# Five small moves in a fused two-block transformer kernel: accumulator banks for one pair of weight chunks, a later broadcast of 1/rms, later loads of gain rows, two head scalings in a row

## The reference

```python
def rmsnorm(x, g, eps=NORM_EPS):
    y = x32 * lax.rsqrt(jnp.mean(x32 * x32, axis=-1, keepdims=True) + eps)
    return (y * g.astype(jnp.float32)).astype(x.dtype)

def swiglu(h, w_up, w_down):
    gate, up = jnp.split(h @ w_up, 2, axis=-1)
    return (jax.nn.silu(gate) * up) @ w_down

# first_block, layer 0: the very first work of the program
x = x + 0.5 * swiglu(rmsnorm(x, norm_g[i, 0]), ffn_w_up[i, 0], ffn_w_down[i, 0])
...
return rmsnorm(x, final_norm_g)          # end of the first block

# second_block
h = rms_norm(x, g_pre_mix[l])            # a norm of a norm
proj = h @ w_in[l]
mq, mk, mv, rq, rk, rv, rg = jnp.split(proj, SPLIT_POINTS, axis=-1)
...
ro = retention(rq, rk, split_heads(rv, RET_HEADS))
ro = ro * lax.rsqrt(jnp.mean(ro * ro, axis=-1, keepdims=True) + NORM_EPS)
ro = jax.nn.silu(rg) * merge_heads(ro).astype(x.dtype)
mix = jnp.concatenate([mo, ro], axis=-1) @ w_out[l]
x = x + rms_norm(mix, g_post_mix[l])
...
x = x + rms_norm(c, g_post_cross[l])
h = rms_norm(x, g_pre_ffn[l])
```

## Time and profile before

| what | value |
|---|---|
| median of 3 runs | 1496.78 us |
| profiled execution | 1497.63 us |
| its span (first to last instruction) | 1495.8 us |
| PE busy | 1458.8 us (98%), 7412 matmuls |
| DVE, ACT, POOL busy | 829.6, 689.0, 45.0 us |
| chain that ended last | PE 95%; ACT, DVE, DMA, SPq 1% each |
| DMA | 262.14 MB, mean 175 GB/s |

### The profile page before, as it was taken

The page is one execution under the profiler, slowest core; times in us unless marked ns, Lnnn a source line. Parts: engine busy times, 40 slices in busy tenths (PEclk is TensorE's granted clock), DMA queues, the critical chain, the costliest instruction groups (busy, mean ns, idle before and its releaser), DMA issues.

```text
span 1495.8 us, 18732 instructions
## 1 busy us (share of the span) xinstructions
PE 1458.8 (98%) x7412; PEld 1228.4 (82%) x7412; DVE 829.6 (55%) x927; ACT 689.0 (46%) x899; POOL 45.0 (3%) x96
## 2 busy tenths in 40 slices
PE   7999999999999999999999999999899999899997
PEld 5888889988888888888888788888787889688886
DVE  4554566855545555445666465545765555454554
ACT  5455354454443544435445454344443444444342
POOL 1000000000000000000000000000101100000000
PEclk9999999999999999999999999999999999899999
DMA  9555554445555455554543356554433544255551
GB/s 353 221 197 181 188 177 169 160 169 197 197 186 184 165 200 195 191 181 163 172 152 128 113 197 235 187 197 169 155 113 117 179 168 142 99 197 181 187 195 57
DMA packets 38574, 262.14 MB, mean 175 GB/s; under 512 B 4288, under 2 KB 4544, under 8 KB 7648
## 3 DMA queue, kind: packets, MB, share of 16 engines
q1 hardware_dynamic: 37152, 252.85, 48.0%
q0 software_dynamic: 1344, 8.16, 1.4%
HBM read 259.95 MB, written 1.05 MB: 174 GB/s over the span
## 4 chain that ended last, share of the span: by engine, by line
PE 95%; ACT 1%; DVE 1%; DMA 1%; SPq 1%; issue 1%; POOL 0%; DVEq 0%; POOLq 0%; ACTq 0%
PE prod L994 15%; PE prod L996 15%; PE prod L995 15%; PE acc L994 9%; PE acc L996 9%; PE acc L995 9%; PE prod L988 4%; PE prod L989 4%; PE prod L990 4%; PE acc L1160 2%; PE aux L1024 2%; DMA raw<-in_weights_dram 1%; PE acc L1011 1%; PE acc L1179 1%; ACT acts_h L1311 1%
## 5 line engine op out<-in xcount | busy, mean ns | idle before, releaser
L1481 DVE TENSOR_TENSOR w_lo<-raw,w_hi 128x2048 fp32r<-128x2048 f32 x235 | 538.4, 2292 | 334.6 <-ACT w_hi L1293 334.3
L1293 ACT CAST w_hi<-raw 128x2048 fp32r<-128x2048 f32 x235 | 449.1, 1912 | 294.8 <-PE acc L996 184.3
L994 PE MATMUL prod<-w_hi,acts_h 128*128 128x512 f32 x960 | 383.6, 400 | 10.5 <-DVE four L1596 7.0
L996 PE MATMUL prod<-w_hi,acts_l 128*128 128x512 f32 x960 | 376.0, 392 | 0.0
L995 PE MATMUL prod<-w_lo,acts_h 128*128 128x512 f32 x960 | 375.7, 391 | 0.0
L994 PE MATMUL acc<-w_hi,mix_h 128*128 128x512 f32 x600 | 237.5, 396 | 2.7 <-DVE sq L1766 2.4
L996 PE MATMUL acc<-w_hi,mix_l 128*128 128x512 f32 x600 | 234.2, 390 | 0.0
L995 PE MATMUL acc<-w_lo,mix_h 128*128 128x512 f32 x600 | 234.2, 390 | 0.0
L994 PEld LDWEIGHTS prod<-w_hi,acts_h 128*128 128x128 f32 x960 | 181.4, 189 | 52.6 <-issue 9.6
L996 PEld LDWEIGHTS prod<-w_hi,acts_l 128*128 128x128 f32 x960 | 181.1, 189 | 38.6
L995 PEld LDWEIGHTS prod<-w_lo,acts_h 128*128 128x128 f32 x960 | 181.6, 189 | 35.8 <-issue 0.5
(11 more groups left out here) (248 smaller groups left out, 1194.5 us busy)
## 6 DMA issues: line engine op xcount, KB each, us to landing
raw<-in_weights_dram SPq DMA_DIRECT2D x235, 1024.0 KB, 4.9
raw<-in_weights_dram SPq DMA_DIRECT2D x12, 256.0 KB, 7.0
work<-in_mem_dram POOLq DMA_DIRECT2D x2, 1024.0 KB, 13.3
grow<-in_gain_rows_dram POOLq DMA_DIRECT2D x4, 512.0 KB, 3.8
tabs<-in_tabs_dram POOLq DMA_DIRECT2D x1, 1696.0 KB, 8.8
work<-in_x_t_dram SPq DMA_DIRECT2D x4, 256.0 KB, 5.9
x_res<-in_x_dram SPq DMA_DIRECT2D x1, 1024.0 KB, 8.7
work<-in_mem_t_dram POOLq DMA_DIRECT2D x1, 1024.0 KB, 14.3
```

The source lines that it names most:

```text
L994: pe.matmul(out, still_hi, wh, start=first, stop=False, skip_group_check=True)
L996: return pe.matmul(out, still_lo, wh, start=False, stop=last, skip_group_check=True)
L1293: act.copy(w_hi[:, c % RING], raw[:, c % RAW]).then_inc(hi_done, 1)
L1481: dve.tensor_tensor(w_lo[:, c % RING], raw[:, c % RAW], w_hi[:, c % RING].bitcast(F32), ALU.subtract).then_inc(lo_done, 1)
```

## The change

Five edits. First, chunks 2 and 3 write `acc[2]` and `acc[3]` in place of the product banks (`up_bank`), chunk 2 no longer waits for a free bank, and the down chunk 4 waits for `mid_done` 4 before it writes `acc[2]`; with this, x is loaded behind the quarters of chunk 2 and squared behind their rounding. Second, at the double norm the spread stands amid the "k" chunk. Third, POOL issues the load of the next gain row behind the next statistic in place of ahead of it (three of four loads; the one at the first statistic stays). Fourth, `late` issues all scales that are due (`while` for `if`). Fifth, `scale_x` stands ahead of the `rg` chunks.

```diff
-        if self.scales < self.sums and not self.hold:
+        while self.scales < self.sums and not self.hold:
             self.pl.head_scale(...)
             self.scales += 1
...
     pl.project(w, 0, "q", 0)
-    pl.spread("x")
-    pl.project(w, 512, "k", 0)
+    pl.project(w, 512, "k", 0, mid=lambda: pl.spread("x"))
...
     pl.ready_v(ret)
+    pl.add("scale_x", stat=pl.stat)
     pl.project_tokens(w, 2560, "rg", 0, mid=slot, between=lambda: end(slot))
     norms.hold = False
     end(slot)
-    pl.add("scale_x", stat=pl.stat)
...
+        def up_bank(it, t):
+            return acc[2 + t] if it["c"] in (2, 3) else prod_flat[(it["e"] + t) % 2]
...
             # SyncE
-            sp.dma_start(x[:], A["x"]).then_inc(x_loaded, 16)
             for k in range(4):
                 sp.dma_start(raw[:, 2, quarter(k)], weights[2][:, quarter(k)])...
+            sp.dma_start(x[:], A["x"]).then_inc(x_loaded, 16)
...
             # GpSimd
                 if kind == "stat":
                     statistic(it)
+                    if next_row:
+                        done, count, row = next_row
+                        pool.wait_ge(done, count)
+                        pool.dma_start(grow[:], A["gain_rows"][row]).then_inc(gain_row_loaded, 16)
+                        next_row = None
...
                 elif kind == "second_squares":
-                    pool.wait_ge(xf_done, 4)
-                    pool.dma_start(grow[:], A["gain_rows"][1]).then_inc(gain_row_loaded, 16)
+                    next_row = (xf_done, 4, 1)
                 elif kind == "post_sums" and it["row"] < 3:
-                    pool.wait_ge(y_copied, it["y_copied"] + 4)
-                    pool.dma_start(grow[:], A["gain_rows"][it["row"] + 1]).then_inc(gain_row_loaded, 16)
+                    next_row = (y_copied, it["y_copied"] + 4, it["row"] + 1)
...
             # TensorE
-                    if k_half == 0:
+                    if k_half == 0 and it["c"] != 2:
                         reader(pe, it["free"][t])
-                        mm = token_passes(prod_flat[e % 2], ...)
+                        mm = token_passes(up_bank(it, t), ...)
...
+                    if b == 2 and it["c"] == 4:
+                        pe.wait_ge(mid_done, 4)
...
             # ScalarE, first_prep (Silu and DVE's product read up_bank too)
+                    for k in range(4):
+                        split_piece(2, k)
+                    state["split"] = RAW
                     act.wait_ge(x_loaded, 16)
                     for b in range(4):
                         ins = square(x[:, t, cols], b, 0)
-                    for k in range(4):
-                        split_piece(2, k)
-                    state["split"] = RAW
```

More of the change, by code:

```diff
@@ L1049, in tokens_chunk @@
                 for t in parts:
-                    e = it["e"] + t
-                    if k_half == 0:
+                    if k_half == 0 and it["c"] != 2:
                         reader(pe, it["free"][t])
@@ L1058, in tokens_chunk @@
                             piece_ready(it["c"], k)
-                        mm = token_passes(prod_flat[e % 2], slot, k * 512, hi[:, base + kt, tokens(t)],
+                        mm = token_passes(up_bank(it, t), slot, k * 512, hi[:, base + kt, tokens(t)],
                                           lo[:, base + kt, tokens(t)], kt == 0, kt == KT - 1)
@@ L1345, in _ @@
                                 act.wait_ge(mid_done, 2 * m + t - 1)
-                            act.activation(gate_s[:, t], prod_flat[(it["e"] + t) % 2][:, 0:S], ACT.Silu,
+                            act.activation(gate_s[:, t], up_bank(it, t)[:, 0:S], ACT.Silu,
                                            scale=rstd["x"][:, t:t + 1]).then_inc(silu_done, 1)
@@ L1596, in _ @@
                             dve.scalar_tensor_tensor(
-                                out=mid_tok[m % 2][:, t], in0=prod_flat[(it["e"] + t) % 2][:, S:2 * S],
+                                out=mid_tok[m % 2][:, t], in0=up_bank(it, t)[:, S:2 * S],
                                 scalar=rstd["x"][:, t:t + 1], in1=gate_s[:, t], op0=ALU.mult, op1=ALU.mult
```

## The result

The changed kernel takes 1478.75 us (median of 4 runs, 1478.37 to 1480.98); the kernel before, timed again beside it, 1497.48 (4 runs, 1493.32 to 1499.19). The ratio is 0.9875, 95% interval 0.9863 to 0.9887: faster by 1.1 to 1.4%. The forecast was 1481.7, so the direction and the range (1476 to 1489) held. The sum said 15.1 us gained; 18.7 were, from 1497.48. The profiled execution took 1478.86 us, its span is 1477.0. One execution of the kernel before in a later session, 2442.22 us at a granted clock of 0.556, belongs to a slow state and is left out of every comparison.

A forecast was written before the change was run, and what follows sets the result against it. PE, busy 98% of the span, bounds the kernel, its waits costing twice through the clock. 5.1 + 4.4 + 1.6 + 4.0 = 15.1 us off 1497.63 gives 1482.5, the median 0.85 lower: 1481.7; range 1476 to 1489.

The forecast's parts named there:

- Banks: First FFN: with other banks for chunk 2, pair 0's transpose starts 7.1 us earlier; 5.1 taken, ends 0 and 7.1.
- If the gap of 2.0 us lowers the clock, as that of 1.8 did, 2.0 us are lost again: First FFN, PE's new gap ahead of pair 0's transpose: a lower clock loses 2.0 us, leaving 5.1.
- 1/rms at 24.4: First FFN: squares end at 22.5, POOL's last operation 1.9 us behind; 1/rms at 24.4, before ACT is free at 24.60.
- Spread: Double norm: spread amid "k" cuts PE's wait from 4.60 to 1.7 us; 4.4 gained if the clock holds, else 2.9.
- Gain rows: Norm behind the cross attention: POOL starts 1.6 us earlier, PE waits 4.0 for 5.6; 1.6 gained, 0 elsewhere.
- Heads: End of retention: both scales early, so PE's 2.4 us wait and 1.6 of low clock go; 4.0 gained.
- The port: Double norm: DVE and POOL share an SBUF port pair exclusively, so moving the load gains 0; without the rule about 1.2.
- Supply: Rival, first FFN: x, squares and 1/rms late, or later weight chunks no sooner; 4 us lost, 1485.7; chance 0.14.
- Load in place of port: Rival, double norm: the load slowed the statistic, not DVE's remainder; spread 1.2 us earlier, 1480.5; chance 0.08.
- No wait over 1 us appeared between 1060 and 1180: Sign for the second block: such a wait would make the forecast wrong; new-wait rival 1490.1, chance 0.07.
- the clock never stayed low: Rival, first FFN: PE stays at 1.2 GHz behind the new 2.0 us gap, slower than before, 1512.7; chance 0.03.

The follow-up runs named there:

- e4: The changed kernel with one scale a slot again (`if` for `while`), scale_x still early; 1482.28 us.
- e2: The changed kernel with the spread ahead of "k" again at the double norm; 1484.29 us.
- e7: The changed kernel with DVE's remainder beside POOL's first operation at the double norm cut into four instructions of 512 columns; 1478.79 us.
- e10: The changed kernel with scale_x behind the scales of heads 0 and 1 again; 1478.73 us.
- e12: The changed kernel with the edits of e8 and e9 together; 1475.49 us.
- e8: The changed kernel with 14 unread 128x512 matmuls in PE's 4.0 us wait at the norm behind the cross attention; 1475.92 us.
- e3: The changed kernel with the gain rows loaded ahead of the statistics again; 1480.88 us.
- e9: The changed kernel with DVE's whole remainder at the double norm put behind POOL's statistic; 1476.73 us.
- e5: The changed kernel with banks kept, but x loaded and squared ahead of chunk 2's quarters as before; 1480.35 us.
- e1: The changed kernel with its first edit undone whole: chunks 2 and 3 in product banks, x loaded and squared ahead of chunk 2; 1486.36 us.
- e6: The changed kernel with the new load order kept, but chunks 2 and 3 in the product banks; 1485.11 us.

## Why the prediction was right, and where its size was off

Undone singly the parts cost 7.6, 5.5, 2.1 and 3.5 us in the medians, together 18.7, and the whole change brought 18.7. That these agree so well is partly luck. In the stages and waits that the edits touch, the four cost 6.7, 4.2, 1.6 and 2.4, together 14.9; the rest is clock in places that the edits leave alone, and e4 leaves `scale_x` early, so it isn't the whole of the two edits at retention. What bears the argument is each place by itself:

1. **Banks** (forecast 5.1, measured 7.6 at the double norm, 1036.47 for 1044.07, and 6.7 when undone alone). The mechanism was right to the wait: chunk 2 without a wait, a gap of 2.0 (2.15) at `turn_mid`, chunk 5 in time. The term that was mis-sized is "If the gap of 2.0 us lowers the clock, as that of 1.8 did, 2.0 us are lost again". It didn't in this profile, and that it didn't is chance. Of nine executions with that gap in their profile (after, e2 to e4, e7 to e10, e12) it fell in three, e2, e8 and e12, and its price there was 1.5 to 1.6, not 2.0. The other half microsecond is the product, which ends at 27.06 in place of the forecast 27.71, since chunk 3 could be rounded 0.66 earlier. That is scatter of the first loads too: over these nine kernels the transpose starts between 26.81 and 28.10, always 7.7 to 7.8 behind chunk 2, which starts between 19.07 and 20.39. The forecast had 1/rms at 24.4, with POOL's last operation as slow as before; it came at 23.4, and nothing waited for it.
2. **Spread** (4.4, measured 4.4: 12.01 less the 7.60 from the banks). The clock held behind 1.69 us, here and in all eight other kernels with a gap of 1.7 to 1.9 there: all have 3.41 to 3.43 from spread to rope.
3. **Gain rows** (1.6, measured 1.74 up to the transposes; 0 at the double norm, measured 0). Another 0.76 came in the stage behind the transposes, 6.82 for 7.58, which the forecast had left at zero. It swings with the clock there (6.82 to 7.92 in kernels that still wait), so it isn't shown to belong to the change.
4. **Heads** (4.0, measured 4.25). The while loop alone does it all (e10), and `scale_x` does nothing beside it. Undone alone the loop costs 2.39 in its stage (e4), not 4.25: the wait of 2.12 is back, but the clock held behind it. Of the 1.86 between e4 and before, 0.28 is the shorter wait and nearly all the rest the clock, which may hold or fall behind such a gap. The reason I gave for the wait of before, `scale_x` and a remainder between the scales, was half right: the remainder makes nearly all of it.
5. **The port.** The rule of the Trainium skill (SBUF — State Buffer, "SBUF: two separate sides") by which I took 0 at the double norm holds: e3 shows the 0, e9 the other side of it, 1.18 us for moving DVE's instruction out of the way. The e7 trace shows that the rule says too little about parts back to back.
6. **Rivals.** Supply: chunk 5 landed in time with the new order, and late without it (e5), so the danger was real and the second half of the first edit removed it. Load in place of port: refuted by the changed kernel itself, where POOL's first operation took 1.38 with no load ahead of it, and by e9. No wait over 1 us appeared between 1060 and 1180, and the clock never stayed low.

In sum 15.1 was forecast and 18.8 measured in the profiles: 2.5 from the banks, 0.8 behind the cross attention's transposes, 0.3 from retention, 0.1 from the rows. So the forecast's direction, places and waits were right by its mechanism; that its sum was 3.6 short is, for 2.0, the toss of the clock in one place.

## What to carry to other kernels

Cut the trace at events that every version has and compare stage by stage: parts of 1 us then show singly in one profile, where medians of runs scatter by 2. Look at the clock of each stage before you put a difference down to an edit. When a wait goes, work out the next one on the same engine and the loads that it will lean on; a bank that is free earlier is worth little if the slot behind it is freed late. A long wait of TensorE that can't be removed can be filled with unread matmuls (1.8 to 2.9 us at a wait of 4.0; nothing measurable at waits of about 2). A long VectorE operation with two inputs in SBUF belongs behind, not beside, a small GpSimd chain that TensorE waits for (1.2 us here).

## What the runs showed of the hardware that I had not expected

- The same gap doesn't always bring the same clock. At mem_v PE waited 1.80 to 1.83 us in 13 kernels; the clock fell behind it in six profiled executions (before, after, e2, e7, e10, e12) and held in seven (e1, e3 to e6, e8, e9). In e12 the window behind it:

```profile
1203.00:1206.00 3.00, 3.00 (x9) 2.29 (x9) 2.45 (x2) 0.00 (x0) 0.00 (x0) 0.53 1.00 396
```

  Behind the 2.1 in the first FFN it was three of nine, behind the 1.7 to 1.9 at the spread none of nine. It held behind 2.12 (e4, retention) and 2.24 (e5, chunk 4) and fell behind 2.40 (before); behind 3.6 to 5.6 it was low each time, in e4 only from about 2 us after the gap. A fall behind a gap near 2 us costs about 1.6 us. For such gaps a forecast should take a share of it, not all or nothing.
- The scatter of the kernel before goes with that clock. Over the four sessions its eight runs with a mean granted clock of 0.993 took 1492.86 to 1494.36 us, and its other 21, at 0.987 to 0.992, took 1496.22 to 1499.93.
- GpSimd's operation ends 0.05 us behind DVE's remainder, whenever it started. At 1041.77 of after the first operation of the other statistic took 0.72 and ended at 1042.49, DVE's remainder at 1042.44. In before ten operations of POOL that began beside a whole remainder ended 0.05 to 0.06 behind it, at lengths from 0.69 to 2.27.
- Cutting that VectorE instruction into four back to back doesn't by itself let GpSimd in: its operation still ended 0.05 us behind the last part (e7). In the first FFN of before it did come in between four parts.
